# One weight tile at a time, and a ReLU that stays in its PSUM banks, in a hybrid attention block

## The reference

```python
proj = x @ W_in                                   # 2048 x 1024 @ 1024 x 2756, split into groups
# group A: per block of 128 queries
dots  = einsum('bqhd,bsd->bqhs', qi_blk, ki)      # 4 index heads
score = einsum('bqh,bqhs->bqs', w_blk * idx_scale, relu(dots))
_, idx = top_k(where(visible, score, -inf), 256)  # each query keeps 256 keys
p = softmax(q . k_sel / 8 - slope * dist)         # 8 heads, 1 shared key/value head
ya = p @ v_sel
# group B: window of 128 keys, 8 heads, with sinks and ALiBi
y = concat(ya * silu(ga), yb * silu(gb)) @ W_out
x = layer_norm(2 ** 0.25 * x + y, g, b)
```

## Time and profile before

| | |
|---|---|
| median of 3 runs | 1483.08 us (1482.07 to 1483.55) |
| profiled execution | 1486.23 us |
| its span, first to last instruction | 1484.4 us |
| mean granted TensorE clock | 0.963 |
| busy: PE, DVE, ACT, POOL | 1368.8, 1171.2, 947.4, 536.8 us |
| projection, to its last product | 0 to 580.2 us |
| attention | 580.2 to 1299.8 us |
| output projection and norm | 1299.8 to 1484.4 us |

### The profile page before, as it was taken

One profiled execution on the slowest core, in us unless ns is written; L12 is line 12 of the kernel. 1 busy time (PEld: TensorE's weight loads), 2 busy tenths in 40 slices (PEclk: granted clock), 3 DMA queues, 4 the chain that ended last, 5 costly groups with the idle time before them and its releaser, 6 DMA issues.

```text
span 1484.4 us, 18616 instructions
## 1 busy us (share of the span) xinstructions
PE 1368.8 (92%) x6004; PEld 993.8 (67%) x6052; DVE 1171.2 (79%) x2407; ACT 947.4 (64%) x1879; POOL 536.8 (36%) x342
## 2 busy tenths in 40 slices
PE   6999999989899897788999999998999788999997
PEld 5887877777688775565555565555555455678886
DVE  3377889677989779888998999898999977347665
ACT  3485876774498636988954799875789966710010
POOL 1323142751441444444331234132113577524332
PEclk9999999999999998698999999999999999999999
DMA  7313132432231237535241122312001043134442
GB/s 250 99 59 120 57 114 68 156 104 67 71 114 58 94 91 165 132 86 116 69 114 57 44 68 71 72 50 81 25 15 54 22 140 95 57 106 156 142 140 87
DMA packets 106544, 136.83 MB, mean 92 GB/s; under 512 B 6642, under 2 KB 83382, under 8 KB 106190
## 3 DMA queue, kind: packets, MB, share of 16 engines
q1 hardware_dynamic: 93296, 93.23, 22.8%
q10 hardware_dynamic: 9504, 31.66, 5.5%
q0 software_dynamic: 3648, 10.76, 2.4%
HBM read 92.20 MB, written 42.34 MB: 91 GB/s over the span
## 4 chain that ended last, share of the span: by engine, by line
PE 62%; ACT 12%; DVE 12%; POOL 6%; issue 5%; DMA 3%; SPq 0%; ACTq 0%; POOLq 0%; DVEq 0%
PE psum L1325 18%; PE psum L1524 11%; PE psum L1475 9%; ACT above L1150 5%; PE psum L1399 4%; PE psum L1462 3%; PE psum L1463 3%; DVE above L1613 3%; PE psum L1461 2%; POOL w_lo L942 2%; PE psum L1356 2%; PE psum L1341 2%; PE psum L1358 2%; POOL w_hi L934 1%; ACT accept L1156 1%
## 5 line engine op out<-in xcount | busy, mean ns | idle before, releaser
L1613 DVE TENSOR_SCALAR_CACHE_REDUCE above<-dist,trial 128x512 bf16<-128x512 int32 (+13 forms) x224 | 345.7, 1543 | 5.8
L1150 ACT ACTIVATE above<-dist,trial 128x384 bf16<-128x384 int32 (+13 forms) x224 | 280.8, 1254 | 21.4 <-DVE trial L1600 8.5
L1325 PE MATMUL psum<-x_hi,w_hi 128*128 128x512 f32 x640 | 255.8, 400 | 34.1 <-POOL w_lo L942 17.4
L1325 PE MATMUL psum<-x_lo,w_hi 128*128 128x512 f32 x640 | 253.4, 396 | 0.0
L1325 PE MATMUL psum<-x_hi,w_lo 128*128 128x512 f32 x640 | 253.3, 396 | 0.0
L1259 ACT ACTIVATE prob<-psum 128x512 f32<-128x512 f32 x272 | 158.4, 592 | 103.8 <-PE psum L1475 50.7
L1715 DVE CUSTOM_DVE_ANT_0 junk<-psum,mask 128x512 bf16<-128x512 f32 (+3 forms) x320 | 184.3, 606 | 29.6 <-PE psum L1399 18.9
L1475 PE MATMUL psum<-prob,vw 128*65 128x512 f32 x376 | 186.7, 601 | 2.3 <-ACT out_a L1100 2.3
L934 POOL CAST w_hi<-raw 128x1024 fp32r<-128x1024 f32 x40 | 54.0, 1350 | 329.0 <-PE psum L1325 323.9
L1462 PE MATMUL psum<-qa_mix,ka_mix 128*128 128x512 f32 x272 | 162.9, 599 | 4.2 <-DMA qa_ext<-minus_max 1.8
L1325 PEld LDWEIGHTS psum<-x_hi,w_hi 128*128 128x128 f32 x640 | 122.8, 192 | 64.7 <-POOL w_lo L942 20.9
(11 more groups left out here) (157 smaller groups left out, 2889.7 us busy)
## 6 DMA issues: line engine op xcount, KB each, us to landing
raw<-w_tiles SPq DMA_DIRECT2D x40, 512.0 KB, 3.8
proj<-staged ACTq DMA_DIRECT2D x40, 512.0 KB, 3.2
qb_raw<-proj SPq DMA_DIRECT2D x32, 256.0 KB, 4.2
qa_raw<-proj SPq DMA_DIRECT2D x32, 256.0 KB, 4.5
yt_raw<-y_t SPq DMA_DIRECT2D x16, 512.0 KB, 5.2
x_row<-x_res SPq DMA_DIRECT2D x16, 512.0 KB, 4.0
out<-z ACTq DMA_DIRECT2D x16, 512.0 KB, 2.6
x_raw<-xT SPq DMA_DIRECT2D x12, 512.0 KB, 3.9
```

The source lines that it names most:

```text
L1150: nc.scalar.activation(above[:, 0, 0:n], src, ACT.Sign, scale=-1.0, bias=u, accum_out=count[:, 0:1]).then_inc(sign_counted, 1)
L1325: last = pe.matmul(psum[:, 2 * u + m, :], wt[:, u, k, :], xt[:, k, 512 * m:512 * m + 512], start=(k == 0 and q == 0), stop=(k == KT - 1 an ...
L1613: v.tensor_scalar(above[:, 1, 0:n], src, u, None, ALU.is_ge, ALU.add, accum_out=count[:, 1:2]).then_inc(own_counted, 1)
```

## The change

Four edits and a new table. The products of a tile, from the third tile of a half on, now need the whole tile before, so that tiles follow one another. For pairs 1 to 5 the ReLU is written over its input in PSUM, and the sums read it there; the bank is then free only after the sum, so TensorE's next dots in this bank wait for `summed`, while ScalarE waits for nothing but the dots. Pairs 6 and 7 keep the SBUF tile. The plan's model follows this, with an assumed duration of the sums of pairs 6 and 7 that is a fifth longer. The table `PREFER`, which ranks the pieces, has other numbers throughout, so that the order of the whole kernel is new.

```diff
-PREFER = {'above': -11609.2, 'band0': -7907.4, 'band1': 3177.2,
+PREFER = {'above': -16961.5, 'band0': -160183.0, 'band1': -51126.0,
...
@@ whole_plan, dots_of
-            add("PE", 4 * (w / 2400 + 0.014), "dots", *part, holds=lock, until=("relu", *part),
+            add("PE", 4 * (w / 2400 + 0.014), "dots", *part, holds=lock, until=("relu" if bank_lock else "sum", *part),
...
-            add("DVE", 0.25 + 1.05 * w / 512, "sum", *part,
+            add("DVE", 0.25 + (1.25 if bank_lock else 1.05) * w / 512, "sum", *part,
@@ whole_plan, products
-        if k == KT - 1 and n:
+        if n and (k == KT - 1 or (k == 0 and t > 1)):
             needs.append(("product", *tiles[n - 1], KT - 1))
@@ whole_plan
-    last_relu = ("relu", *last_dots[0][1:])
+    last_relu = ("sum", *last_dots[0][1:])
@@ hybrid_kernel
+        def weighed(p, h, bank, w):
+
+            return psum[:, bank:bank + 2, 0:w] if p < NPAIR - 2 else relu[:, h:h + 2, 0:w]
@@ index_relu
-                if n_dots >= 2:
+                if p >= NPAIR - 2:
                     act.wait_ge(summed, 2 * (n_dots - 1))
...
-                nc.scalar.activation(relu[:, h:h + 2, 0:w], psum[:, bank:bank + 2, 0:w], ACT.Relu,
+                nc.scalar.activation(weighed(p, h, bank, w), psum[:, bank:bank + 2, 0:w], ACT.Relu,
@@ index_dots
-                read_last[bank] = (relued, n_dots + 1)
+                read_last[bank] = (summed, 2 * n_dots + 2) if p < NPAIR - 2 else (relued, n_dots + 1)
@@ unit_logits
-                    pe.wait_ge(relued, 2 * chunks_before(NPAIR - 2))
+                    pe.wait_ge(summed, 4 * chunks_before(NPAIR - 2))
@@ index_sum
+                both = weighed(p, h0, 4 + h0 if p < NPAIR - 2 else 2, w)
...
-                        v.tensor_scalar(o, relu[:, h, 0:w], wt, 0.0, ALU.mult, ALU.add).then_inc(summed, 1)
+                        v.tensor_scalar(o, both[:, h - h0, :], wt, 0.0, ALU.mult, ALU.add).then_inc(summed, 1)
...
-                        v.scalar_tensor_tensor(o, relu[:, h, 0:w], wt, o, ALU.mult, ALU.add).then_inc(summed, 1)
+                        v.scalar_tensor_tensor(o, both[:, h - h0, :], wt, o, ALU.mult, ALU.add).then_inc(summed, 1)
```

2 lines of the change are left out of this document (1 added, 1 removed).

## The result

The changed kernel took 1492.58 us in the median of 4 runs (1491.31 to 1494.02), the kernel before 1483.09 (1482.07 to 1483.55) beside it: a ratio of 1.0065, 95% interval [1.0048, 1.0083]. It is slower, outside the predicted range and on the side of rival 3. The profiled execution took 1494.02 us with a span of 1492.2, 7.8 us more than that of the kernel before.

A forecast was written before the change was run, and what follows sets the result against it. TensorE's idle and slow time, with VectorE's chain, was taken to bound the kernel. TensorE's projection lead of 10 us and small sum gains gave -9 us: profiled 1486.2 to 1477.2, median 1474 us; forecast 1467 to 1479, full range 1456 to 1491.

The forecast's parts named there:

- rival 3: Banks held until the sum and the chain winning nothing back make the kernel slower: +10 us, 1493 us; chance 0.23.
- waits and clock: In the projection, TensorE's waits for GpSimd's split weights go (-19 us) with the clock lost behind them (-8.5 us).
- new waits: TensorE's third dots of pairs 2 to 5 wait for sums: +25 us, plus 3 us of slow clock.
- contention: VectorE's sums with a PSUM input escape slowing by GpSimd: 8 us taken, between none and 14.
- what goes is covered by nothing else: Removed weight waits of TensorE in the projection count in full, 19 us and 8.5 us of clock.
- the chain has to win that back: The index starts 20 us late; VectorE's sums, sort and search recover, with pair 5's first count at 571.5 us.
- less 5 for faster sums: Pair 2 to pair 3 on VectorE: 93.3 us from sum to sum shrinks by 5, to 232.5 us.
- The lead at the attention: TensorE ends the projection 10 us earlier, VectorE's chain 3 us; 8 or 9 of the 10 carry into the attention.
- rival 1: VectorE's chain decides in the attention, so only its 3 us carry: 1481.5 us; chance 0.14 together with Rival 4.
- The attention's order: The new succession of attention pieces was taken at 0, within 11 us either way; work behind the last masks unchanged.
- rival 2: The attention's new succession is better than the old, losing 15 us less behind the projection: 1459 us; chance 0.21.
- Rival 4: GpSimd's splits remain the limit because ScalarE's tile copies hold the bank: today's time; chance 0.14 together with rival 1.

The follow-up runs named there:

- number 1: Kernel before, only with the products from the third tile of a half on taken tile by tile, ReLU in SBUF: 1471.6 us, ratio 0.9909.
- number 9: number 1 with the first half's eight norm groups moved ahead, behind the first nine products, so the index starts late: 1492.9 us, ratio 1.0063.
- number 5: Changed kernel in its new order throughout, but with the ReLU of pairs 1 to 5 written to SBUF: 1486.8 us, ratio 1.0018.
- number 13: number 1 with all eight norm groups of the second half alone ahead of the second tile's end: 1489.6 us, ratio 1.0047.
- number 14: First half of the projection as in number 1, then second half and attention in the new order, ReLU in SBUF: 1479.2 us, ratio 0.9971.
- number 6: Changed kernel with the first half's norm groups moved back, two behind the third tile, six behind pair 1's dots: 1492.8 us, ratio 1.0055.
- 7: Changed kernel with the second half's norm groups moved back, two behind the second tile, six behind pair 4's dots: 1502.0 us, ratio 1.0118.
- number 4: Changed kernel's order and PSUM ReLU up to the last product of the projection, then the order of the kernel before: 1487.8 us, ratio 1.0022.
- number 3: Order of the kernel before up to the last product of the projection, then the changed kernel's order, ReLU in SBUF: 1504.3 us, ratio 1.013.

## Why the prediction was wrong

**The sum as measured.** From 1483.1: tiles in sequence -12 (number 1), a late start of the index +21 (number 9 against 1), the rest of the new order -6 (number 5 against 9; groups of the second half, other places, the attention), the ReLU in PSUM +6 (changed against 5). These steps lead from one kernel to the next, so they must end at the 1492.6 measured; the agreement proves nothing by itself. And a step's size depends on what surrounds it. The groups of the second half cost 18 us in number 13 and lie here within the -6. The late start costs 21 us in the old order, while the first half's whole order costs 7.6 us in the new one (number 14 against 5), and putting its groups back gained the changed kernel nothing in the median (number 6). I had -27.5 for waits and clock, +28 for new waits, 0 for the late start, 0 for the ReLU less 8 of contention, and 0 for the attention.

**Tile by tile: the waits went, and a third of the term came.** I took 19 us of waits and 8.5 us of clock away, and said that what goes is covered by nothing else. TensorE's waits for w_lo on the matmul row are 2.1 us after and 1.0 in number 1. Yet number 1, which has this part alone, ends the projection 8.5 us earlier, not 27.5. Other waits grew by 9.4 us in their place, and the clock gave nothing back: the sum of 8.5 us for it was of three windows, and TensorE's busy time over the whole projection is the same with and without these waits. That no split of 6 us would be left was wrong too, and it mattered: one of 6.4 us delays the queries of pair 5 in number 1.

**The ReLU in PSUM: durations nearly right, the place of its cost wrong.** ScalarE took 1008 ns in place of 1025. The first sum took 750 ns (I had 680), the others 751. None was over 754 ns, beside a longest of 2769 from SBUF, so the contention went as forecast: the 128x512 sums take 98.8 us of VectorE in the changed kernel (its four groups 49.6, 26.0, 16.5, 6.7) and 109.6 in number 5, 10.8 less, where I had put 8. In the kernel before and in number 5 each of the sums over 0.9 us, 16 and 18 of 152, ran while a GpSimd instruction ran; of the 104 from PSUM 26 did, and none is slow. The Trainium skill, "SBUF — State Buffer", section "SBUF: two separate sides", names a port pair that VectorE, in a two-port mode or with two SBUF inputs, and GpSimd lock against each other for a whole instruction; the trace agrees, by those 754 ns. The Trainium skill, "VectorE: DVE Perf Modes", section on the TRN2 errata, would give a PSUM sum 658 ns as an estimate; the trace has 750, and the measurement decides. What I left out is that a bank now passes TensorE, ScalarE and VectorE in series. I priced this as 25 us of waits of TensorE, and in the changed kernel these stayed small (9.7 us). It fell on VectorE's chain, where the sums of a pair take up to 3.8 us longer. In two pairs of kernels it cost 5.8 and 13.3 us; in the second pair TensorE's waits grew as well (21.5 us against 13.9).

**The failing step: "the chain has to win that back".** The first dots came at 77.3 us, as I had them (76.0). I gave the chain 144.5, 232.5, 350 and 532.7 us for the first sums of pairs 2 to 5 and 571.5 for pair 5's count; it came to 149.0, 243.3, 364.3, 537.5 and 587.6, so that the count is 13 us later than before and not 3 us earlier. From first sum to first sum, "less 5 for faster sums" made 88 us of pair 2 to 3; it was 94.3, one more than before. From pair 5's first sum to its count I had 39 us and there were 50.1 (before: 48.1), with sums 33.9 us apart and a sort step that took 5.92 us instead of 3.89. And I let the two late starts act through TensorE's counts of products alone, where the list also ties ScalarE's copies of tiles to its counts (numbers 6, 7). By pair 5's first sum the chain had won back some 10 of its 21.6 us, and only between pairs 4 and 5; two of these were lost again by the count. That the start is what the chain carries is shown by number 9 for number 1's order; how much of it the changed kernel carries by itself stays open (7.6 us is what number 14 has for the whole first half).

**The lead at the attention: wrong weight.** I gave the attention 8 or 9 of TensorE's 10 us, because it is as busy as VectorE. From the first count of pair 5 to the output projection the traces have 717 to 726 us in 16 of 17 kernels; from the end of the projection it is 713 to 737 in all. These ranges decide little, because among kernels with the same attention TensorE's lead over the count hardly varies: 11 us with the new one, -6 or -7 with the old. The kernels that do vary it are two. Number 4 has 13 us more with the old attention, which gained 1.6 us. Number 3 lacks 17 us with the new one, and there it takes 741 us from the count, 15 to 24 above the others with this attention. By these two, a lead beyond what the order uses is worth almost nothing, and one that it needs is worth nearly all of itself. With the first count at 587.6 these 717 to 726 us alone give an output projection at 1305 to 1314; rival 1 named the rule but took my own milestone for it.

**The attention's order: a term put at nothing.** I wrote that the work behind the last masks is the same to two pieces, and counted value pieces. Two of group B's window pieces had moved there too. The stretch takes 113.0 us in place of 109.4, and 107.7 with the old attention behind the same projection; that is the 5 us of number 4.

**The rivals.** Rival 3 named 1493 and "if the chain wins nothing back", and the time is its own. But its place was not: pair 5's first sum came at 537.5 us, below the 541 it gave, and the third dots waited 2.8 us, not 29; that the time agrees is luck. The attention's new order, rival 2, is not better but 5 us worse than the old one (number 4). Rival 4, GpSimd's splits as the limit, fell with number 1, whose time is not today's, though one slow split still holds up TensorE there. The forecast's own mark, a projection that ends at 570 us while the last masks still come at 1190, is close to what happened, at 576.4 and 1194.6 us.

## What to carry to other kernels

Where one list fixes the order of five engines, find the chain that cannot be overtaken (here sums, sort and search, pair after pair) and price an edit by what it does to that chain's first link; in number 9 a start that was 21 us late stayed 21 us late to the end. The engine that leads gains little by leading more: 13 us bought 1.6 (number 4), while 17 us too few cost 15 or more (number 3). A buffer held for one stage longer is priced by the period of the loop that runs through it, and not only by the wait of the engine that asks for it. When pieces are reordered, count all the kinds that cross a milestone, not the commonest one. And a new order that brings four things at once may hide a good edit: one of them alone, with four sets of dots moved that had waited in front of ready work, made the kernel 1.5% faster, while together they made it slower. Price each wait that you remove by what stands behind it: of 16 us of waits for weights 9 came back as waits for something else.

## What the hardware showed that I had not expected

- A tensor_scalar from PSUM took 750 ns for 128x512 float32, one from SBUF 483 to 486 at the median; scalar_tensor_tensor took 751 or 752 from either. Beside GpSimd the SBUF forms reached 2.8 us (kernel before, number 5); no PSUM form passed 0.76, though 26 of 104 ran beside it.
- ScalarE's ReLU back into PSUM took 1008 ns in place of 1025 for 128x1024. The Trainium skill, "ScalarE: Activation LUTs", section "Step-by-step: what each stage is for", has PSUM as the faster destination; the trace agrees, by 17 ns.
- Two stalls of TensorE of 4.4 and 5.0 us came with a granted clock of 0.90 over 70 us, which is a mix of full speed and the half level of 1.2 GHz; without them the clock was 1.00 over the same stretch, and the projection gained 12.7 us for 9.4 us of stalls.
